# Slot transposes ahead of later modulation transposes, and the first gather in two halves around the first expert product

## What is computed

```python
def _expert_choice_ffn(h, w_router, w_gate, w_up, w_down):
    b, n, d = h.shape
    cap = EC_FACTOR * n // N_EXPERTS
    aff = jax.nn.softmax(jnp.einsum('bnd,de->bne', h, w_router).astype(jnp.float32), axis=-1)
    g, idx = lax.top_k(jnp.swapaxes(aff, 1, 2), cap)
    xg = jax.vmap(lambda hb, ib: hb[ib])(h, idx)
    hid = jax.nn.silu(jnp.einsum('becd,edf->becf', xg, w_gate)) * jnp.einsum('becd,edf->becf', xg, w_up)
    out = jnp.einsum('becf,efd->becd', hid, w_down) * g[..., None].astype(h.dtype)
    return jax.vmap(lambda ob, ib: jnp.zeros((n, d), ob.dtype).at[ib.reshape(-1)].add(ob.reshape(-1, d)))(out, idx)
...
        mc = _modulation(c_ctx[None], w_mod[l], b_mod[l])
        ml = _modulation(c, w_mod[l], b_mod[l])
...
        h = _rmsnorm(xl, norm_ffn[l]) * (1.0 + ml[4]) + ml[3]
        xl = xl + ml[5] * _expert_choice_ffn(h, w_router[l], w_exp_gate[l], w_exp_up[l], w_exp_down[l])
```

## Time and profile before

| | us |
|---|---|
| median of 3 runs | 1969.41 |
| lowest and highest | 1968.26, 1969.76 |
| the profiled execution | 1969.08 |
| its span, first to last instruction | 1967.2 |
| PE busy | 1850.7 (94%) |
| DVE busy | 631.4 (32%) |
| ACT busy | 348.2 (18%) |
| HBM read | 547.54 MB |

### The profile page before, as it was taken

How to read it: one execution, slowest core, us unless ns; L and a number is a source line. 1 busy time by engine, 2 the same in 40 slices (tenths; PEclk the granted TensorE clock), 3 DMA queues, 4 the chain that set the end, 5 groups by cost and what they waited for, 6 DMA issues and landing times.

```text
span 1967.2 us, 19769 instructions
## 1 busy us (share of the span) xinstructions
PE 1850.7 (94%) x8226; PEld 928.9 (47%) x8226; DVE 631.4 (32%) x1236; ACT 348.2 (18%) x815; POOL 57.7 (3%) x43
## 2 busy tenths in 40 slices
PE   7999999999999988898899999999999999888887
PEld 3565566555544333233265555665556343333323
DVE  2633356455221111111155233655533112111112
ACT  3223231000121010010132242210002010101102
POOL 0200000000100000000002000000000000000000
PEclk9999999999999999999999999999999999999999
DMA  9515251442799999999992244216336999999996
GB/s 390 199 69 214 92 218 44 171 171 77 276 397 427 426 429 427 428 427 427 412 377 97 86 179 169 97 43 257 116 151 255 428 427 427 428 428 426 429 426 277
DMA packets 54841, 553.03 MB, mean 281 GB/s; under 512 B 5984, under 2 KB 9952, under 8 KB 13280
## 3 DMA queue, kind: packets, MB, share of 16 engines
q1 hardware_dynamic: 50976, 549.13, 67.3%
q10 hardware_dynamic: 3776, 2.62, 0.4%
HBM read 547.54 MB, written 4.19 MB: 280 GB/s over the span
## 4 chain that ended last, share of the span: by engine, by line
PE 71%; DMA 28%; ACT 0%; DVE 0%; issue 0%; SPq 0%; DVEq 0%; ACTq 0%
PE psum L1230 14%; PE psum L1014 13%; PE psum L885 12%; DMA ring<-in_w_up 8%; DMA dense<-in_w_down 8%; DMA ring<-in_w_gate 8%; PE psum L887 6%; PE psum L1098 6%; PE psum L1123 4%; DMA dense<-in_w_gate 4%; PE psum L421 2%; PE psum L847 2%; PE psum L933 1%; PE psum L1200 1%; PE psum L867 1%; PE psum L972 1%
## 5 line engine op out<-in xcount | busy, mean ns | idle before, releaser
L1014 PE MATMUL psum<-hT,ring 128*128 128x384 f32 x768 | 255.8, 486 | 0.0
L1230 PE MATMUL psum<-ring,dense 128*64 128x512 f32 x960 | 216.0, 595 | 29.0 <-DMA ring<-in_w_gate 17.8
L885 PE MATMUL psum<-hT,ring 128*128 128x384 f32 x720 | 238.8, 487 | 0.0
L1014 PEld LDWEIGHTS psum<-hT,ring 128*128 128x128 f32 x768 | 145.6, 190 | 100.9
L1230 PE MATMUL psum<-dense 128*64 128x512 f32 x704 | 162.1, 606 | 25.5 <-DMA dense<-in_w_gate 18.6
L885 PEld LDWEIGHTS psum<-hT,ring 128*128 128x128 f32 x720 | 135.0, 190 | 90.7 <-issue 1.4
L1230 PEld LDWEIGHTS psum<-ring,dense 128*64 128x64 f32 x960 | 68.2, 137 | 167.9 <-issue 138.8
L1937 DVE TENSOR_TENSOR state<-state,psum 128x512 f32<-128x512 f32 x32 | 22.0, 688 | 371.1 <-PE psum L1230 333.1
L1098 PE MATMUL psum<-dense,ring 128*128 128x384 f32 x384 | 131.9, 487 | 0.0
L887 PE MATMUL psum<-ring,hT 128*128 128x512 f32 x288 | 126.5, 594 | 0.0
L1850 DVE RECIPROCAL kcT<-kcT 128x384 f32<-128x384 f32 x48 | 122.6, 2553 | 1.7
(11 more groups left out here) (237 smaller groups left out, 1689.3 us busy)
## 6 DMA issues: line engine op xcount, KB each, us to landing
dense<-in_w_gate SPq DMA_DIRECT2D x34, 2048.0 KB, 35.9
ring<-in_w_in SPq DMA_DIRECT2D x60, 1024.0 KB, 9.9
ring<-in_w_up SPq DMA_DIRECT2D x30, 2048.0 KB, 37.7
ring<-in_w_gate SPq DMA_DIRECT2D x30, 2048.0 KB, 36.1
wide<-in_w_up SPq DMA_DIRECT2D x22, 2048.0 KB, 37.6
dense<-in_w_down SPq DMA_DIRECT2D x20, 2048.0 KB, 39.7
ring<-in_w_mod SPq DMA_DIRECT2D x38, 1024.0 KB, 8.9
ring<-in_w_down SPq DMA_DIRECT2D x18, 2048.0 KB, 39.9
```

Of the source, the lines that this page charges most:

```text
L885: last = M.matmul(psum[:, bank, 0:T], ring[:, n % RING, k, cols], hT[:, k, :], start=k == 0, stop=k == KD - 1)
L1014: last = M.matmul(psum[:, Z[1], 0:T], ring[:, n_gate % RING, k, (j % 4) * P:(j % 4 + 1) * P], hT[:, k, :], start=k == 0, stop=k == KD - 1)
L1230: last = M.matmul(psum[HALF * half:HALF * (half + 1), bank, :], lhsT(k), SPARE_BLOCKS[2 * kk + half] if spare else w[:, kk, half * SLAB:(h ...
```

## The change

There are three edits, all in the stretch between the router and the first expert product.

1. In layer 0 the chain order becomes product A, product B, product C, transposes A, transposes B, transposes C. Before it was product A, product B, transposes A, product C, transposes B, transposes C. `EARLY_CHAIN[0]` goes from 5 to 4, so transposes B now stand behind the slot transposes. Both late transposes use bank S[1], and the second therefore waits until the first has been read.
2. Transposes C of layer 0 stand behind G0 instead of ahead of it, and ACT reads them between its two halves of the first gather.
3. In both layers G1 no longer follows G0. The order is G0, P0, G1, P1. Later groups still gather both halves in a row.

```diff
-                return steps + [("mod",) + m[2], ("modT",) + m[1], ("modT",) + m[2]]
+                return steps[0:2] + [("mod",) + m[2], ("modT",) + m[0], ("modT",) + m[1], ("modT",) + m[2]]
...
-        EARLY_CHAIN = [5, 4]
+        EARLY_CHAIN = [4, 4]
...
-                        pe.wait_ge(z_read, max(f_of("mod", l, j) + 1, f - 1))
+                        same_bank = filler_bank(f) == filler_bank(f - 1)
+                        pe.wait_ge(z_read, max(f_of("mod", l, j) + 1, f if same_bank else f - 1))
...
-                        fill(CHAIN_FILL[layer][EARLY_CHAIN[layer]:])
+                        fill(CHAIN_FILL[layer][EARLY_CHAIN[layer]:EARLY_CHAIN[layer] + 1])
...
+                        gather_half(0)
+                        if quad:
+                            gather_half(1)
...
-                        product(expert, 0, S[0], gate_h, gathered_chunk(expert))
+                        product(expert, 0, S[0], gate_h, gathered_chunk(expert), (lambda: gather_half(1)) if expert == 0 else None)
...
                     gather(0)
+                    fill(CHAIN_FILL[layer][EARLY_CHAIN[layer] + 1:])
                     gate_product(0)
...
-                    read(CHAIN_FILL[layer][EARLY_CHAIN[layer]:])
+                    read(CHAIN_FILL[layer][EARLY_CHAIN[layer]:EARLY_CHAIN[layer] + 1])
...
+                            if quad == 0 and part:
+                                read(CHAIN_FILL[layer][EARLY_CHAIN[layer] + 1:])
```

More of the change, by code:

```diff
@@ L1195, in gather, with gather_half @@
                             pe.wait_ge(sc_read, at(sc_read, KD * (quad - 1)))
[L1196 to L1206, removed]
+                        gather_half(0)
+                        if quad:
+                            gather_half(1)
+                    def gather_half(half):
+                        chunks = range(4 * half, 4 * half + 4)
+                        for k in chunks:
+                            for b in (1, 2):
+                                last = M.matmul(psum[:, XG[half], (k % 4) * P:(k % 4 + 1) * P], x_rows[:, b, k * P:(k + 1) * P],
+                                                pick[:, b].rearrange("p e s -> p (e s)"), start=b == 1, stop=b == 2)
+                        last.then_inc(xg_full, 1)
+                        for k in chunks:
+                            last = M.matmul(psum[:, XG[2 + half], (k % 4) * HALF:(k % 4 + 1) * HALF], x_rows[:, 0, k * P:(k + 1) * P],
+                                            pick[:, 0, :, 0:CAP_CTX], start=True, stop=True)
+                        last.then_inc(xg_full, 1)
                     def product(expert, s0, bank, signal, lhsT, between=None):
```

## The result

| | before | after |
|---|---|---|
| median, us (10 runs each) | 1968.91 | 1974.18 |
| lowest and highest | 1968.26, 1969.86 | 1972.94, 1975.43 |
| span of the profiled execution | 1967.2 | 1971.8 |
| HBM read, MB | 547.54 | 547.54 |
| mean granted clock | 0.998 | 0.998 |

The ratio is 1.0027, with a 95% interval of 1.0019 to 1.0036. The change costs 5.3 us, and by its interval it is slower. That is 3 us more than the 1971.2 of the forecast. It lies outside the case that the forecast added up (1970.5 to 1972.8) and only 0.1 us inside its full range (1967.9 to 1974.3), which had been widened for rivals. That it hit is luck.

A forecast was written before the change was run, and what follows sets the result against it. The prediction took the full DMA queue of slab loads to bound the kernel. A later restart at entry 10, 0.65 + 1.32 = +1.97 us, gave 1971.2 us; summed case 1970.5 to 1972.8, full range 1967.9 to 1974.3.

The forecast's parts named there:

- What bounds the kernel: In both expert stages the full DMA queue sets the end: its beginning plus its bytes at 428 GB/s.
- Parts 1 and 2: Layer 0 before P0: new order starts G0 0.68 us earlier; transposes C, 0.66 us, are hidden behind G0.
- only the slots count: Rival: if splitting the gather left the queue unchanged, layer 0's new order alone gives 1968.7; chance 0.14 shared with halfway cases.
- Part 3: G1 behind P0, both layers: P0 starts 4.10 us after G0, P1 7.63 us after P0 instead of 3.43.
- The second hole: Queue runs dry again before late entry 10; its stream starts 0.65 us later in layer 0, 1.32 in layer 1.
- third dip: Drop in DMA share at entry 12; the forecast expected none and named it a sign of being wrong.
- Entry 12: Load waiting for expert 1's first product: issued 0.5 us late in both layers, cost taken as zero, 0.5 kept for the range.
- the ramp of a lone load: A load starting alone: queue moves 262 instead of 428 GB/s over its first 1.5 us, losing 0.58 us.
- the turn: Moment, in issue times, when the loads ahead of an entry are done, at 4.90 us per load.
- PE's delay in full: Rival: PE's lateness of 2.12 and 2.79 us moves the stage ends fully, +4.91 us, to 1974.2; chance 0.10.
- The clock falls: Rival: P1 after idle PE runs at 1.2 GHz, entry 10 comes 1.75 us later per layer, 1974.7; chance 0.08.
- The queue profits after all: Rival: entry 10 reaches the queue before entry 9 is done, ends move by P0's gains, -3.49 us, 1965.7; chance 0.06.

The follow-up runs named there:

- run 4: Kernel before with nine unused matmuls on PE behind the first product of expert 1, both layers; 1969.46 us beside 1969.12, ratio 1.0004.
- run 7: Kernel before with five unused matmuls between P2 and the product on slab (0,3), both layers; 1971.99 us beside 1969.23, ratio 1.0017.
- run 10: Kernel before with layer 0's new chain order, gather in a row, entries 9 and 12 each loaded in two halves; 1970.36 us beside 1969.08, ratio 1.0007.
- run 3: Kernel before with five unused matmuls on PE between P0 and P1, both layers; 1974.18 us beside 1969.12, ratio 1.0023.
- run 1: Kernel before with only layer 0's new chain order, transposes C ahead of the gather, both gather halves in a row; 1969.24 us beside 1969.12, ratio 1.0000.
- run 11: Kernel before with new layer 0 order, transposes C in bank S[0], gather in a row, five dummy matmuls for eight in layer 1; 1967.94 us beside 1969.23.
- run 6: Changed kernel with six of eight matmuls on slab (0,3) left out in both layers; 1971.27 us beside 1969.08, ratio 1.0012.
- run 2: Kernel before with G1 moved behind P0 in layer 1 only; 1971.79 us beside 1969.12, ratio 1.0014.

## Why the prediction was right in its course and short in its sum

**What bounds the kernel: right in the main.** PE could be 2.35 us late behind product (1,0) at no cost (run 4), while 0.5 us at entry 12 cost 2.8 (run 7). The stream of slabs sets the end. But the end isn't just the queue's beginning plus its bytes at 428 GB/s: by the count of run 10 the changed kernel has lost 1.69 and 2.83 us at 410 us behind product B, of the 1.87 and 3.63 by which its stages grew, run 3 1.58 and 1.63 of 3.26 and 2.42. In the undisturbed stages this rest is at most 0.4.

**Parts 1 and 2: right.** G0 0.71 us earlier for 0.68, transposes C hidden. What I had not seen is that part 1 alone would bring nothing (run 1): the table load on ACT stands between the two reads. My case "only the slots count" at 1968.7 could not have come from the chain order alone. It takes part 2, or another bank as in run 11.

**Part 3: right to a tenth.** 4.18 for 4.10 us, 7.76 for 7.63.

**The second hole: right in place, a little small.** Forecast +0.65 and +1.32, together 1.97. The changed kernel without its third dip (run 6) gives +2.2 by the medians, +0.97 and +1.95 by the stage lengths. Most of the difference comes from distances 0.03 to 0.13 us away from the forecast: with the measured 7.76, and P0 earlier by 2.03 and 1.32 relative to product B, the same formula gives 0.83 and 1.54, together 2.37.

**Entry 12: the step that failed.** I had its lateness right, 0.5 us in both layers, and then took its price as zero, with 0.5 as a bound. The argument was that the ramp of a lone load (262 GB/s over 1.5 us) pushes the turn back. The runs say otherwise. The same lateness alone costs 2.8 us for both layers (run 7), and its removal from the changed kernel gives back 3.1 (run 6). The mistake was to apply the ramp only to the restart at entry 10 and not to entry 12 itself. When the queue has worked off nearly all it holds, the next load brings a ramp of its own: 246 GB/s for 2 us in run 7, which is (428 - 246) / 428 x 2 = 0.85 us, and 0.25 us more in the two stretches behind it (410 and 393 GB/s). These 1.1 us hold the lateness too: 0.49 plus the 0.58 of the forecast's own ramp. The cost of being late isn't the lateness but the lateness plus a restart, and, by the count of run 10, 0.4 to 0.6 us more that shows only at the end of the stage (which grew by 1.75 and 1.37). With run 7 as an independent price, 2.2 + 2.8 = 5.0 of the 5.3 us are accounted for.

**The rivals.** *PE's delay in full* named 1974.2, the time that came, and even entry 12 as the place. Its mechanism is refuted all the same: by it, run 4 should have cost 4.7 us, and it cost 0.3. That +4.91 and +5.3 are close is a coincidence of two sums. *The clock falls*: the clock was 1.00 ahead of and in P1. *The queue profits after all* would have needed entry 10 within 4.90 us of entry 9. (The 4.03 us that the prediction sets against it are the way from G0's start to the end of the reads, matmuls included; the reads themselves take 1.10 and 1.50.)

**What stays open.** By layer the parts don't add up well: in layer 1 the third dip costs 1.68 us (443.29 - 441.61), in layer 0 0.90 (441.83 - 440.93), whereas the pad of run 7 gives 1.37 and 1.75. These are single executions, and undisturbed stages scatter by up to 0.45. Layer 1's +3.6 came twice (the changed kernel and run 2), so part of it is likely real. By the count of run 10, 0.80 and 1.2 us of it arise only where the queue runs out; the cause of that part is not shown. Nor is why entry 10 on its turn costs about 1.1 us a layer in run 3.

## What to carry to other kernels

Where a queue of loads is fed by freed buffers, one early release brings nothing unless the next releases follow within one transfer time: write down each issue against its turn, for several entries behind the change. Count a place where the queue empties at its lateness plus a restart (here together some 1.1 to 1.4 us for 0.5 us of lateness), and treat a slack smaller than a few tenths as none. By the traces, to move the whole row of releases forward by half a microsecond was worth more than to move the first one by two; the times alone don't show that gain.

## What I had not expected of the hardware

- Lateness is paid with a multiple. In the kernel before, 0.8 us of PE delay ahead of entry 12 cost 0.55 us in both layers together, 1.5 us of it cost 2.8.
- A transfer that meets a nearly emptied queue runs slowly for about 2 us (246 GB/s in run 7, 287 in the changed kernel), although the DMA share is 0.71 and 0.77. With two halves of 1 MB, 1.7 us apart, the rate was 332 to 365 GB/s for 8 us.
- Part of a disturbance early in a stage is paid 400 us later. Run 10 had moved more bytes than the kernel before at 410 us behind product B, and its last product came 0.87 and 1.37 us later, behind a queue that took over 6 us to run out in layer 1 and not 4.
- Behind ACT's table load of 1.28 us its next instruction started at once (544.31 + 1.28 = 545.59, start 545.60 in run 1). What hurt was where the load stood, ahead of a read that PE needed.
